# Two blocks of a network on one core: the feed-forward layer takes tokens before their norm, and three projections become split fp32r products

## The chip, the cores and the metric

The program runs on 1 core of a Trainium2 chip, as one launch. The metric is the device time in microseconds (us) of that core, as the median of several runs.

## The reference, cut to what matters

256 tokens of 1024 features go through two different blocks. The first block mixes tokens (a stick-breaking attention and a gated linear attention, called gla) and then has a convolutional feed-forward layer:

```
y = (jax.nn.sigmoid(gate_sb + b_gate[0]) * (o_sb @ w_branch_sb)
     + jax.nn.sigmoid(gate_gla + b_gate[1]) * (o_gla @ w_branch_gla))
h = h + y @ w_out                      # [256, 1024]
hn = rms_norm(h, norm_ffn_g)           # h * rsqrt(mean(h*h) + eps) * g, per token
u = hn @ w_ffn_in                      # [256, 2 * 2816]
a, g = jnp.split(u, 2, axis=-1)
a = causal_depthwise_conv(a, conv_w, conv_b)
h = h + (jax.nn.gelu(a) * g) @ w_ffn_out
```

The second block norms its input, projects it (`w_in_2`, a part of 416 columns called lat and a part of 512 columns called u), attends, and ends in a mixture of experts: 32 experts, the best 4 for each token, weights `w_gate_up_2` (8.4 MB an expert) and `w_down_2` (4.2 MB an expert), all in fp32.

## The kernel before, in words

Everything is written out by hand: each engine has its own program, and semaphores order them. `tensor_program` is TensorE's (PE), `vector_program` VectorE's (DVE), `scalar_program` ScalarE's (ACT), `gpsimd_program` GpSimd's (POOL), and `sync_program` issues the weight loads (SP). The weights of the first block and of the second block's projections come in pieces of 1 MB (128 x 2048 fp32) through a ring of 6 slots; a piece is loaded when the product that used the slot's last piece is done. Results are written to the 8 banks of PSUM in the order of the tables `RESULTS` and `RESULTS2`.

A *split product* replaces one fp32 product by three fp32r ones. ACT rounds the weights (`w_hi`, `ff_hi`), DVE or POOL subtracts to get what is left (`split_lo` into `ring_r`, `ffn_lo` into `ff_lo`), the same is done with the other operand, and PE adds hi*hi + hi*lo + lo*hi. Before the change the first 20 pieces (`SPLIT = 20`, the input projection) and the feed-forward layer are done so. The two branch projections (`branch(f, q)`, 8 column blocks `f` by 2 branches `q`, L1899) and the output projection (`project`, L1699) are plain fp32.

The stages around the change are, in time:

1. Branch projections from 152.8 us, gating into `y_T` on DVE (L1210 to L1213), output projection into banks `wo00` to `wo11`.
2. `h` gets the result (L1221), is transposed on PE (`turn_quarter`, banks `hT..`), drained with the gain (L1012). DVE and ACT form the mean of squares, POOL the reciprocal root. The factor of each token must be laid along the free dimension: DVE makes a diagonal (`h_diag`), PE multiplies it by ones (bank `rb1`), DVE multiplies `h_nT` by the bank (L1251), ACT rounds (`h_hi`, L809), DVE and POOL subtract (`h_lo`). `awake` issues 9 and then 6 matmuls that compute nothing, between these waits.
3. The feed-forward layer has 11 steps (`FF_STEPS`) of 256 columns. Step i needs `ffn_in("a", i)` and `ffn_in("g", i)` (48 matmuls of 256 columns each), then on ACT and DVE the chain pad, convolution (6 operations), gelu, product `ff_u`, `u_hi`, `u_lo`, and `ffn_out(i)` (24 matmuls of 512 columns into banks 0 to 3). PE's order in the loop is a(i+1), out(i), g(i+1).
4. After `ffn_out(10)` the four banks are added to `h`, transposed (`nT..`), and go through lat (2 x 8 matmuls of 416 columns) and u (32 of 256). The norm factor for u is broadcast through bank `rb` between lat and u. On ACT and DVE the lat values are scaled, their norms taken, and PE goes on with `qlT` when `lat_ready` says so.
5. Attention, router, and the experts. The first expert loads wait for results of the attention (L391: bank `pm1`).

Of the kernel before, what the change touches and what calls it, by code (L numbers as in the profile page):

```python
# [62 lines left out]
SPLIT = 20  # L63
# [159 lines left out]
def build(nc, w, out):  # L223
    with ExitStack() as ctx:
# [257 lines left out]
def gpsimd_program(g, pool):  # L482
# [146 lines left out]
def scalar_program(g, act):  # L629
# [31 lines left out]
    def w_hi(n):  # L661
# [126 lines left out]
    def ffn_step(i, q, turns, i0):  # L788
        pad(i, q)
        if i0 + 1 < FF_STEPS:  # L790
            ffn_hi("a", turns, i0 + 1)
        gelu(i, q)
        ffn_hi("o", turns, i0)
        if i0 + 1 < FF_STEPS:
            ffn_hi("g", turns, i0 + 1)
# [5 lines left out]
    act.wait_ge(s.y_ready, KT)  # L801
    ffn_hi("a", 0, 0)
    ffn_hi("g", 0, 0)
    square("ffn", *r1.drained("wo10"), scratch=t.ff_u[:].rearrange("p q k n -> p (q k n)"))
    act.preload_act_table(ACT.Gelu_apprx_tanh)
    for h in range(2):
        for b in range(NB):
            act.wait_ge(s.h_normed, 2 * h + b + 1)
            act.activation(h_part(t.h_hi, b, h), h_part(t.h_nT, b, h), ACT.Copy).then_inc(s.h_rounded, 1)  # L809
    act.wait_ge(s.ff_zero, 1)  # L810
# [149 lines left out]
def vector_program(g, dve):  # L960
# [228 lines left out]
    sb_out(1)  # L1189
    dve.wait_ge(*r1.drained("og1"))  # L1190
# [32 lines left out]
    def ffn_lo(kind, i, i0):  # L1223
# [3 lines left out]
        if i0 > 0:  # L1227
            dve.wait_ge(s.ff_a if kind == "a" else s.ff_o, i)
        dve.tensor_tensor(t.ff_lo[:, "ago".index(kind), :], t.ring[:, slot, :], t.ff_hi[:, slot, :].bitcast(F32),
                          ALU.subtract).then_inc(s.ff_lo_dve, 1)  # L1230

    add_mixed(0, 0)
    ffn_lo("a", 0, 0)
    add_mixed(0, 1)
    add_mixed(1, 0)
    for b in range(NB):
        turned("hT", t.h_nT, "norm_ffn", b, 0)
    add_mixed(1, 1)
# [1519 lines left out]
```

## Time and profile before

| | us |
|---|---|
| median of 3 runs | 1455.63 (1455.58 to 1460.12) |
| the profiled execution, its own time | 1460.94 |
| its span, first to last instruction | 1459.2 |
| PE busy in the span | 1386.4 |
| DVE, ACT, POOL busy | 676.2, 287.8, 518.4 |
| mean granted clock of TensorE | 0.989 of full |

The profile gives for the span busy time by engine, the chain of work that ended last, and groups of instructions; the trace below it gives each instruction. An fp32 matmul stands in PE's timeline as two records, an fp32r one as one. A start is in us from the first instruction of the span.

### The profile page before, as it was taken

What the parts mean: (1) busy time and instruction counts of PE and PEld (TensorE: products, weight loads), DVE (VectorE), ACT (ScalarE), POOL (GpSimd) and SP (SyncE); (2) the same over time, 40 slices, a digit from 0 to 9 for tenths busy, and PEclk for the clock granted to TensorE, in tenths of its full rate; (3) what the DMA queues carried; (4) which work ended last, traced back from release to release, by engine and by line L of the source; (5) the groups of instructions that cost most, each with busy time, mean ns of one, the idle gap of its engine ahead of it and who ended that gap; (6) DMA issues with size and microseconds to landing.
All of it is one profiled execution on the core that took longest, in us unless ns stands there. A gap on an engine that the chain in (4) does not pass through costs nothing.

```text
span 1459.2 us, 21155 instructions
## 1 busy us (share of the span) xinstructions
PE 1386.4 (95%) x7640; PEld 790.1 (54%) x7641; DVE 676.2 (46%) x1124; ACT 287.8 (20%) x445; POOL 518.4 (36%) x532
## 2 busy tenths in 40 slices
PE   8999999999989999999999999999998998999995
PEld 8899848999966753433433433433433333334332
DVE  7664436667646443433433433444434444333233
ACT  5644023444325300010100100000000000001001
POOL 3000012222233245565526556456654655200000
PEclk9999999999999999999999999999999999999998
DMA  9544254555545689999997999999999999999994
GB/s 312 174 145 134 98 173 145 177 196 174 187 147 198 259 346 390 429 429 426 429 428 309 430 427 428 427 429 428 428 427 428 429 426 429 427 429 428 428 427 199
DMA packets 77415, 480.76 MB, mean 329 GB/s; under 512 B 7019, under 2 KB 31272, under 8 KB 52808
## 3 DMA queue, kind: packets, MB, share of 16 engines
q1 hardware_dynamic: 74046, 477.45, 80.8%
q10 hardware_dynamic: 3338, 2.88, 0.7%
q8 instruction: 22, 0.36, 0.1%
q14 instruction: 9, 0.07, 0.0%
HBM read 479.26 MB, written 1.05 MB: 329 GB/s over the span
## 4 chain that ended last, share of the span: by engine, by line
PE 65%; DMA 30%; DVE 3%; issue 1%; ACT 1%; POOL 0%; SPq 0%; POOLq 0%; ACTq 0%; DVEq 0%
DMA ring_b<-in_w_down 22%; PE bank L2227 16%; PE bank L2303 12%; PE bank L1967 8%; PE bank L1749 6%; DMA ring<-in_w_gate_up 5%; PE bank L1979 4%; PE bank L1699 4%; PE bank L2209 2%; PE bank L1899 2%; DMA ring_b<-in_w_gate_up 2%; PE bank L1765 2%; PE bank L2262 1%; PE bank L1689 1%; PE bank L2051 1%
## 5 line engine op out<-in xcount | busy, mean ns | idle before, releaser
L619 POOL COPY ring<-stage 128x1024 f32<-128x1024 f32 x300 | 308.4, 1073 | 318.6 <-DMA stage<-in_w_gate_up 223.9
L2227 PE MATMUL bank<-ring,x_T 128*64 128x512 f32 x1584 | 356.0, 597 | 6.5 <-DMA ring<-in_w_gate_up 6.0
L2303 PE MATMUL bank<-ring_b,act_T 128*64 128x512 f32 x1056 | 244.3, 613 | 31.8 <-DMA ring_b<-in_w_down 31.3
L2227 PEld LDWEIGHTS bank<-ring,x_T 128*64 128x64 f32 x1584 | 112.6, 137 | 226.7 <-issue 210.9
L2303 PEld LDWEIGHTS bank<-ring_b,act_T 128*64 128x64 f32 x1056 | 77.9, 140 | 181.9 <-issue 154.1
L1569 DVE TENSOR_TENSOR h<-h,bank 128x512 f32<-128x512 f32 x128 | 82.3, 684 | 201.5 <-PE bank L2262 201.5
L1545 DVE SCALAR_TENSOR_TENSOR y_lo<-bank,slot_gate,y_hi 128x512 fp32r<-128x512 f32 x33 | 24.8, 751 | 226.3 <-ACT y_hi L900 226.3
L2227 PE MATMUL bank<-ring_b,x_T 128*64 128x512 f32 x528 | 120.6, 599 | 2.3 <-DMA ring_b<-in_w_gate_up 2.3
L914 ACT ACTIVATE sig<-bias_raw 128x512 f32<-128x512 f32 x33 | 20.8, 629 | 463.5 <-DVE bias_raw L1575 463.5
L619 POOL COPY ring_b<-stage_b 128x1024 f32<-128x1024 f32 x100 | 103.8, 1080 | 19.1 <-DMA stage_b<-in_w_gate_up 17.5
L544 POOL TENSOR_TENSOR ff_lo<-ring,ff_hi 128x2048 fp32r<-128x2048 f32 x11 | 51.0, 4640 | 157.8 <-PE bank L1967 111.1
L1967 PE MATMUL bank<-h_hi,ff_hi 128*128 128x256 f32 x352 | 99.9, 284 | 2.2 <-POOL h_lo L551 1.7
L1967 PE MATMUL bank<-h_lo,ff_hi 128*128 128x256 f32 x352 | 99.7, 283 | 0.0
L1967 PE MATMUL bank<-h_hi,ff_lo 128*128 128x256 f32 x352 | 99.7, 283 | 0.0
L900 ACT ACTIVATE y_hi<-bank,slot_gate 128x512 fp32r<-128x512 f32 x33 | 22.7, 687 | 274.5 <-PE bank L2303 274.5
L2227 PEld LDWEIGHTS bank<-ring_b,x_T 128*64 128x64 f32 x528 | 35.0, 136 | 71.3 <-issue 67.2
L624 POOL TENSOR_TENSOR bias_raw<-h,g_rows 128x1024 f32<-128x1024 f32 x1 | 2.4, 2361 | 193.2 <-DVEq L1637 193.2
L1967 PEld LDWEIGHTS bank<-h_hi,ff_hi 128*128 128x128 f32 x352 | 67.6, 192 | 3.1 <-issue 2.1
L786 ACT ACTIVATE ff_hi<-ring 128x2048 fp32r<-128x2048 f32 x33 | 61.8, 1903 | 34.4 <-DMA ring<-in_w_ffn_in 34.4
L2209 PE MATMUL bank<-picks,h_half 128*128 128x128 f32 x512 | 68.1, 287 | 0.0
L1967 PEld LDWEIGHTS bank<-h_lo,ff_hi 128*128 128x128 f32 x352 | 67.6, 192 | 0.4
L1967 PEld LDWEIGHTS bank<-h_hi,ff_lo 128*128 128x128 f32 x352 | 67.6, 192 | 0.0
(446 smaller groups left out, 1886.4 us busy)
## 6 DMA issues: line engine op xcount, KB each, us to landing
stage<-in_w_gate_up SPq DMA_DIRECT2D x75, 2048.0 KB, 24.6
ring_b<-in_w_down SPq DMA_DIRECT2D x64, 2048.0 KB, 23.3
stage_b<-in_w_gate_up SPq DMA_DIRECT2D x25, 2048.0 KB, 25.0
ring<-in_w_gate_up SPq DMA_DIRECT2D x21, 2048.0 KB, 25.0
ring<-in_w_in SPq DMA_DIRECT2D x22, 1024.0 KB, 5.1
ring<-in_w_ffn_in SPq DMA_DIRECT2D x22, 1024.0 KB, 5.1
ring_b<-in_w_gate_up SPq DMA_DIRECT2D x7, 2048.0 KB, 25.5
ring<-in_w_ffn_out SPq DMA_DIRECT2D x11, 1024.0 KB, 4.9
```

What stands on the lines that cost most here:

```text
L544: pool.tensor_tensor(t.ff_lo[:, 1, :], t.ring[:, slot, :], t.ff_hi[:, slot, :].bitcast(F32), ALU.subtract).then_inc(s.ff_lo_pool, 1)
L619: ins = pool.tensor_copy(pair_slot(g, pair)[:, cols], stage_place(g, pair)[:, cols])
L786: act.activation(t.ff_hi[:, n % RING, :], t.ring[:, n % RING, :], ACT.Copy).then_inc(s.ff_hi_done, 1)
L1569: dve.tensor_tensor(t.h[:, b, cols], t.h[:, b, cols], g.banks[2 + c][:], ALU.add).then_inc(s.added, 1)
L1699: ins = pe.matmul(bank[:, 0:n], src[:, k, b * P:(b + 1) * P], wk[:, c0:c0 + n], start=(k == 0), stop=(k == len(weights) - 1))
L1749: ins = pe.matmul(into[f // 2][:, (f % 2) * T:(f % 2 + 1) * T], wt[:, k, f * P:(f + 1) * P], xt[:, 4 * half + k, :], start=((half, part) = ...
L1765: ins = pe.matmul(into[b][:], xt[:, 4 * half + k, b * P:(b + 1) * P], wt[:, k, :], start=((half, part) == (0, 0) and k == 0), stop=((half, ...
L1967: ins = pe.matmul(bank[:, f * T:(f + 1) * T], wt[:, k, f * P:(f + 1) * P], ht[:, k, :], start=(k == 0 and part == 0), stop=(k == KT - 1 an ...
L1979: ins = pe.matmul(banks[2 * b + c][:], ut[:, q, k, b * P:(b + 1) * P], wt[:, k, 512 * c:512 * c + 512], start=False, stop=last, skip_group ...
L2209: ins = pe.matmul(banks[6][:, f * P:(f + 1) * P], t.h_half[:, b, k_rows], t.picks[:, b, :], start=(b == 0), stop=(b == 1))
L2227: ins = pe.matmul(banks[n][rows, :], t.x_T[:, c, :], job_slot(g, c)[:, c0:c0 + 512], start=False, stop=(c == GU - 1), skip_group_check=True)
L2303: ins = pe.matmul(banks[4][rows, :], t.act_T[:, k, SLOTS * (c // 2):SLOTS * (c // 2) + SLOTS], job_slot(g, GU + c)[:, c0:c0 + 512], start= ...
```

## The change: what it does

- **Split products for branches and output.** `SPLIT` becomes 28: pieces 20 to 27 are rounded on ACT (`w_hi`) and subtracted on DVE (`split_lo`). The activations are split as well: `o_hi`/`o_lo`, `gla_hi`/`gla_lo`, `y_hi_T`/`y_lo_T`, ACT rounding and DVE subtracting. PE does three fp32r products in place of each fp32 one. All first-branch blocks but two now come ahead of the transposes `ogt`.
- **Raw tokens.** `h_hi` and `h_lo` are made from `h_nT` without the token's norm factor. The factor is applied to a in the pad operation, which moves from ACT to DVE and multiplies by `h_scale` (a copy of bank `rb1`), and to g after `ffn_out`, when the rows are added to `h`. The diagonal product `rb1` moves in between the halves of the first `ffn_in` products. Both `awake` calls there go.
- **Loop order.** PE does a(i+1), g(i+1), out(i). DVE does `ffn_lo("a", i+1)` first in a step and `ffn_lo("o", i)` last.
- **End of the layer.** The last `ffn_out` is done bank by bank, with the first transposes between, lat starts before the last transpose, and bank `rb` comes between the halves of u.

```diff
-SPLIT = 20
+SPLIT = 28
...
+            act.wait_ge(s.w_split, n - HI + 1)
...
-    for n in range(4, 8):
-        gate(n)
+    gate(4)
+    gate(5)
+    w_hi(20)
+    o_high(0)
+    o_high(1)
+    w_hi(21)
+    gate(6)
+    gate(7)
+    w_hi(22)
     for b in range(NB):
         take(r1, f"og{b}", t.o_gla[:, b, :], r1.bank(f"og{b}")[:])
+    w_hi(23)
+    for n in range(2):
+        gla_high(n)
+    for f in range(3):
+        y_turned_high(f)
+    w_hi(24)
+    y_turned_high(3)
+    w_hi(25)
+    for f in range(4, KT):
+        y_turned_high(f)
+    w_hi(26)
+    w_hi(27)
...
     def ffn_step(i, q, turns, i0):
-        pad(i, q)
         if i0 + 1 < FF_STEPS:
             ffn_hi("a", turns, i0 + 1)
+            ffn_hi("g", turns, i0 + 1)
+        ffn_hi("o", turns, i0)
         gelu(i, q)
...
+        if f >= 1:
+            y_low(f - 1)
         dve.wait_ge(*r1.drained(f"y{f}"))
         dve.tensor_tensor(t.y_T[:, f, :], y_a, y_b, ALU.add).then_inc(s.y_ready, 1)
+    split_lo(24)
+    y_low(KT - 1)
+    split_lo(25)
...
+        if i0 + 1 < FF_STEPS:
+            ffn_lo("a", i + 1, i0 + 1)
+        dve.wait_ge(s.ff_a, i + 1)
+        dve.tensor_tensor(t.a_pad[:, q, :, 2:], g.banks[4 + q][:].rearrange("p (k n) -> p k n", k=2),
+                          t.h_scale[:].unsqueeze(1).to_broadcast([P, 2, T]), ALU.mult).then_inc(s.ff_pad, 1)
...
-        dve.tensor_tensor(t.h[:, b, cols], t.h[:, b, cols], g.banks[2 * b + n][:], ALU.add).then_inc(s.rows_added, 1)
+        dve.scalar_tensor_tensor(out=t.h[:, b, cols], in0=g.banks[2 * b + n][:], scalar=rstd("ffn", b),
+                                 in1=t.h[:, b, cols], op0=ALU.mult, op1=ALU.add).then_inc(s.rows_added, 1)
...
+        for part, (wt, xt) in enumerate(((w_hi, x_hi), (w_lo, x_hi), (w_hi, x_lo))):
+            if f == 0 and part != 1:
+                pe.wait_ge(s.o_rounded if part == 0 else s.o_split, 2 * q + 2)
+            if f % 4 == 0 and part < 2:
+                pe.wait_ge(s.w_rounded if part == 0 else s.w_split, n + 1)
...
+        into = [open_bank(r1, f"wo{col}{b}") for b in blocks]
+        for half, part in ((0, 0), (0, 1), (1, 0), (1, 1), (0, 2), (1, 2)):
+            w_hi, w_lo = split_parts(g, n + half)
+            wt, yt = ((w_hi, t.y_hi_T), (w_hi, t.y_lo_T), (w_lo, t.y_hi_T))[part]
+            if part == 0:
+                pe.wait_ge(s.w_rounded, n + half + 1)
+                pe.wait_ge(s.y_rounded, 4 * half + 4)
...
-            ffn_out(m * 2 + q, q, q)
             ffn_in("g", m * 2 + (q + 1), q + 1, banks[7 - q], s.ff_g)
-    ffn_out(FF_STEPS - 1, FF_STEPS - 1, 0, end=True)
+            pe.wait_ge(s.ff_u, m * 2 + (q + 1))
+            for b, c in QUARTERS:
+                ins = ffn_out(m * 2 + q, q, q, b, c)
+            ins.then_inc(s.ff_o, 1)
```

On PE, from the output projection to the first feed-forward matmuls, the program before reads as follows (`x_n` is the buffer of `y_T`; `ident` alone is an `awake` matmul):

```order
L1699 MATMUL bank<-ring,x_n 128x512 x24
L1677 MATMUL bank<-ident,h 128x128 x8
L1699 MATMUL bank<-ring,x_n 128x512 x8
L1708 MATMUL bank<-ident 128x128 x9
L1943 MATMUL bank<-h_diag,ones 128x128 x2
L1947 MATMUL bank<-zrow 128x512 x4
L1708 MATMUL bank<-ident 128x128 x6
L1967 MATMUL bank<-h_hi,ff_hi 128x256
```

The same place on PE in the changed program, from the second column half's first bank on:

```order
L1751 MATMUL bank<-ident,h 128x128 x8
L2018 MATMUL bank<-w_hi,y_hi_T 128x512 x4
L2018 MATMUL bank<-w_hi,y_lo_T 128x512 x4
L2018 MATMUL bank<-ring_r,y_hi_T 128x512 x8
L1751 MATMUL bank<-ident,h 128x128 x4
L2036 MATMUL bank<-zrow 128x512 x4
L2069 MATMUL bank<-h_hi,ff_hi 128x256 x8
L2069 MATMUL bank<-h_hi,ff_lo 128x256 x8
L2069 MATMUL bank<-h_lo,ff_hi 128x256 x8
L2095 MATMUL bank<-h_diag,ones 128x128 x2
```

The `h_diag` product stood between the output projection and the first feed-forward matmul; it now has three of the four half products (24 matmuls each) of step 0 ahead of it and one behind.

On DVE, where the gated `y` is made, one block `f` before:

```order
L1210 TENSOR_TENSOR gr_e<-bank,gates 128x256
L1211 TENSOR_TENSOR gr_e<-bank,gates 128x256
L1213 TENSOR_TENSOR x_n<-gr_e 128x256
L1214 MEMSET a_pad 128x516
L1215 MEMSET a_pad 128x516
```

and the last block with what follows it now (`y_lo_T` is the low part of the block before):

```order
L1268 TENSOR_TENSOR gr_e<-bank,gates 128x256
L1269 TENSOR_TENSOR gr_e<-bank,gates 128x256
L1260 TENSOR_TENSOR y_lo_T<-x_n,y_hi_T 128x256
L1273 TENSOR_TENSOR x_n<-gr_e 128x256
L1056 TENSOR_TENSOR ring_r<-ring,w_hi 128x2048
```

Each block has four operations in place of three, and weight subtractions stand behind the last.

On PE at the end of the feed-forward layer, before:

```order
L1979 MATMUL bank<-ff_hi,u_lo 128x512
L1677 MATMUL bank<-ident,h 128x128 x16
L1699 MATMUL bank<-ring,h_nT 128x416 x16
L2012 MATMUL bank<-diag,ones 128x128 x2
L1689 MATMUL bank<-h_nT,ring 128x256 x32
```

and now, behind the last quarter of `ffn_out`:

```order
L2081 MATMUL bank<-ff_hi,u_lo 128x512
L1751 MATMUL bank<-ident,h 128x128 x4
L2126 MATMUL bank<-ring,h_nT 128x416 x4
L1773 MATMUL bank<-ring,h_nT 128x416 x8
L2139 MATMUL bank<-h_nT,ring 128x256 x16
L2148 MATMUL bank<-diag,ones 128x128 x2
```

Two of the four transposes have moved ahead of the last quarter, one stands in the middle of the first lat product, and the `diag` product (bank `rb`) is half of u later.

## Rows read from the trace of the kernel before

**Rows 1.** The page: the chain that ended last by engine and line; bandwidth in 40 slices.

```profile
GB/s 312 174 145 134 98 173 145 177 196 174 187 147 198 259 346 390 429 429 426 429 428 309 430 427 428 427 429 428 428 427 428 429 426 429 427 429 428 428 427 199
...
PE 65%; DMA 30%; DVE 3%; issue 1%; ACT 1%; POOL 0%; SPq 0%; POOLq 0%; ACTq 0%; DVEq 0%
```

**Rows 2.** The chain in order of time: start, length, what (x: records).

```profile
36.42 11.09 PE bank L1765 x48
...
92.56 22.77 PE bank L1749 x192
...
160.84 20.72 PE bank L1899 x96
181.56 20.60 PE bank L1699 x48
...
255.79 5.47 PE bank L1979 x24
261.26 11.51 PE bank L1967 x96
...
405.17 7.35 PE bank L1979 x24
...
416.93 11.18 PE bank L1699 x32
428.55 13.81 PE bank L1689 x64
```

**Rows 3.** PE's timeline at the norm: start, busy, line, operation, idle ahead.

```profile
209.74 0.60 PE L1677 MATMUL bank<-ident,h 128*128 128x128 f32 x4
...
214.38 1.03 PE L1947 MATMUL bank<-zrow 1*128 1x512 bf16 x4
...
218.36 0.36 PE L1967 MATMUL bank<-h_hi,ff_hi 128*128 128x256 f32 x1 [1.41 <-POOL h_lo L551]
```

**Rows 4.** PE's timeline before the first and the last `ffn_out`.

```profile
238.59 0.47 PE L1979 MATMUL bank<-ff_hi,u_hi 128*128 128x512 f32 x1 [1.44 <-DVE u_lo L1282]
...
405.17 0.47 PE L1979 MATMUL bank<-ff_hi,u_hi 128*128 128x512 f32 x1 [2.31 <-DVE u_lo L1282]
```

**Rows 5.** Windows: length, busy of PE, PEld, DVE, ACT, POOL; clock, DMA.

```profile
236.00:239.00 3.00, 1.56 (x12) 1.34 (x11) 2.96 (x3) 1.81 (x2) 1.90 (x1) 1.00 0.19 32
...
407.00:410.00 3.00, 3.00 (x10) 2.40 (x9) 0.00 (x0) 0.00 (x0) 0.00 (x0) 0.64 0.00 0
```

**Rows 6.** DVE's timeline, the operations that the change repeats, adds or moves.

```profile
134.28 2.29 DVE L1019 TENSOR_TENSOR ring_r<-ring,w_hi 128x2048 fp32r<-128x2048 f32 x1 [1.63 <-ACT w_hi L667]
...
158.09 1.23 DVE L1199 TENSOR_TENSOR sb_s<-sb_s,rstd 128x1024 f32<-128x1024 f32 x1 [1.86 <-POOL rstd L503]
...
164.34 0.42 DVE L1210 TENSOR_TENSOR gr_e<-bank,gates 128x256 f32<-128x256 f32 x1 [2.60 <-PE bank L1899]
164.79 0.42 DVE L1211 TENSOR_TENSOR gr_e<-bank,gates 128x256 f32<-128x256 f32 x1
...
335.13 0.69 DVE L1279 TENSOR_TENSOR ff_u<-ff_ge,bank 128x512 f32<-128x512 f32 x1 [2.03 <-PE bank L1967]
336.52 3.74 DVE L1282 TENSOR_TENSOR u_lo<-ff_u,u_hi 128x512 fp32r<-128x512 f32 x1 [0.70 <-ACT u_hi L799]
```

**Rows 7.** POOL's timeline in the same loop step, and ACT's at 132 us.

```profile
335.09 4.62 POOL L544 TENSOR_TENSOR ff_lo<-ring,ff_hi 128x2048 fp32r<-128x2048 f32 x1 [12.36 <-PE bank L1967]
...
132.28 1.90 ACT L667 ACTIVATE w_hi<-ring 128x2048 fp32r<-128x2048 f32 x1
```

**Rows 8.** DVE's timeline after the last `ffn_out`.

```profile
412.54 1.88 DVE L1294 TENSOR_TENSOR h<-h,bank 128x512 f32<-128x512 f32 x3 [7.52 <-PE bank L1979]
...
425.93 0.48 DVE L1324 TENSOR_SCALAR diag<-ident,rstd 128x128 f32<-128x128 f32 x2 [2.77 <-POOL rstd L564]
...
437.73 0.35 DVE L1351 TENSOR_SCALAR lat_n<-lat,rstd 128x256 f32<-128x256 f32 x1 [4.30 <-POOL rstd L503]
```

**Rows 9.** SP's waits from 390 to 530 us: total, times, longest.

```profile
SPq L391 <- PE bank L2082: 10.2, 1, 10.2
```

More of the change, by code:

```diff
@@ L1934, in tensor_program @@
         turn_quarter(r1, "hT", t.h, b, 0)
-    project(r1, "wo11", 1, wo, t.y_T, 0, 512)
-    for b in range(NB):
-        pe.wait_ge(*r1.drained(f"wo1{b}"))
-        turn_quarter(r1, "hT", t.h, b, 1)
-    awake(9, 0)
+    mixed_out(1, (1,), 26)
+    pe.wait_ge(*r1.drained("wo10"))
+    turn_quarter(r1, "hT", t.h, 0, 1)
+    pe.wait_ge(*r1.drained("hT10"))
+    for n in range(4):
+        pe.matmul(banks[n][:], t.zrow[0:1, 0:P], t.zrow[0:1, P:], start=True, stop=False)
+    pe.wait_ge(*r1.drained("wo11"))
@@ new lines, in tensor_program, with ffn_parts, ffn_in @@
+    turn_quarter(r1, "hT", t.h, 1, 1)
+    def ffn_parts(kind, i, i0):
+        slot = ffn_chunk(g, kind, i0) % RING
+        pe.wait_ge(s.ff_lo_pool if kind == "g" else s.ff_lo_dve, ffn_made(kind, i)[1])
+        kt = 2 if kind == "o" else KT
+        return (t.ff_hi[:, slot, :].rearrange("p (k m) -> p k m", k=kt),
+                t.ff_lo[:, ffn_rest(kind, i0), :].rearrange("p (k m) -> p k m", k=kt))
+    def ffn_in(kind, i, i0, bank, done):
+        w_hi, w_lo = ffn_parts(kind, i, i0)
+        for f in range(2):
+            for k in range(KT):
+                for part, (wt, ht) in enumerate(((w_hi, t.h_hi), (w_hi, t.h_lo), (w_lo, t.h_hi))):
+                    ins = pe.matmul(bank[:, f * T:(f + 1) * T], wt[:, k, f * P:(f + 1) * P], ht[:, k, :],
+                                    start=(k == 0 and part == 0), stop=(k == KT - 1 and part == 2))
+        ins.then_inc(done, 1)
@@ new lines, in ffn_in_half @@
+    def ffn_in_half(kind, half, bank):
+        w_hi, w_lo = ffn_parts(kind, 0, 0)
+        for part, (wt, ht) in enumerate(((w_hi, t.h_hi), (w_lo, t.h_hi), (w_hi, t.h_lo))):
+            if kind == "a" and part == 0:
+                pe.wait_ge(s.h_rounded, 2 * half + 2)
+            if kind == "a" and part == 2:
+                pe.wait_ge(s.h_split, half + 1)
+                pe.wait_ge(s.h_split_pool, half + 1)
+            for f in range(2):
+                for k in range(4 * half, 4 * half + 4):
+                    ins = pe.matmul(bank[:, f * T:(f + 1) * T], wt[:, k, f * P:(f + 1) * P], ht[:, k, :],
+                                    start=(f == 0 and k == 0 and part == 0),
+                                    stop=(f == 1 and k == KT - 1 and part == 2), skip_group_check=True)
+        return ins
@@ new lines, in ffn_out @@
+    def ffn_out(i, i0, q, b, c):
+        w_hi, w_lo = ffn_parts("o", i, i0)
+        end = i0 == FF_STEPS - 1
+        for k in range(2):
+            for part, (ut, wt) in enumerate(((t.u_hi, w_hi), (t.u_hi, w_lo), (t.u_lo, w_hi))):
+                last = end and k == 1 and part == 2
+                ins = pe.matmul(banks[2 * b + c][:], ut[:, q, k, b * P:(b + 1) * P],
+                                wt[:, k, 512 * c:512 * c + 512], start=False, stop=last,
+                                skip_group_check=not last)
+        return ins
@@ L1940, in tensor_program @@
+    QUARTERS = [(b, c) for b in range(NB) for c in range(2)]
+    ffn_in_half("a", 0, banks[4])
+    pe.wait_ge(*r1.drained("hT11"))
+    ffn_in_half("g", 0, banks[6])
+    ffn_in_half("a", 1, banks[4]).then_inc(s.ff_a, 1)
     pe.wait_ge(s.h_diag_ready, NB)
@@ L1971, in ffn_out @@
-    def ffn_out(i, i0, q, end=False):
-        w_hi, w_lo = ffn_parts("o", i, i0)
-        pe.wait_ge(s.ff_u, i + 1)
-        for b in range(NB):
-            for c in range(2):
-                for k in range(2):
-                    for part, (ut, wt) in enumerate(((t.u_hi, w_hi), (t.u_hi, w_lo), (t.u_lo, w_hi))):
-                        last = end and k == 1 and part == 2
-                        ins = pe.matmul(banks[2 * b + c][:], ut[:, q, k, b * P:(b + 1) * P],
-                                        wt[:, k, 512 * c:512 * c + 512], start=False, stop=last,
-                                        skip_group_check=not last)
-        ins.then_inc(s.ff_o, 1)
```

253 lines of the change are left out of this document (151 added, 102 removed).

## The prediction

> **What bounds the kernel now.** I read the page first. The chain that ended last is 65% PE and 30% DMA [rows 1]. The bandwidth line shows where the two change places: up to the 12th of 40 slices (36.5 us each) the core draws 98 to 312 GB/s, from the 17th on it draws about 428 without a break, one slice excepted [rows 1]. So up to some 510 us the kernel is a chain of products, and behind that it is a stream of expert weights. The change lies wholly in the first part, from 152.8 to 442 us. Does a gain there reach the end? The first expert load waits for a bank of the attention (SP stood 10.2 us before it [rows 9]), so the start of the stream hangs on the front's chain. The stream then moves with it; I take 1 us at the end for 1 us at the front.
>
> Next I read the chain in order of time and PE's timeline beside it. Between 152.8 and 202 us PE is solid with fp32 products. Then come small waits at the norm, waits around the first `ffn_out`, a loop without idle time at 5.47 + 11.51 = 16.98 us a step [rows 2], a wait of 2.31 us before the last `ffn_out` [rows 4], and gaps around the transposes.
>
> **The cost of each product.** A branch matmul (fp32, 256 columns) takes 20.72 us for 96 records, which are 48 matmuls: 0.432 us. An output matmul (512 columns) takes 20.60/24 = 0.858. An fp32r matmul of 256 columns takes 22.77/192 = 0.119, one of 512 columns 11.09/48 = 0.231 [rows 2]. There are 64 branch matmuls and 32 output ones.
> Before: 64 x 0.432 + 32 x 0.858 = 55.1 us. After: 192 x 0.119 + 96 x 0.231 = 45.0. **Term 1: -10.1 us**, if the operands are there in time.
>
> **Are they?** Each of the eight added weight pieces costs ACT 1.90 [rows 7] and DVE 2.29 us [rows 6]. I walked through the changed programs with these durations. Pieces 20 to 22 fit into holes of ACT and DVE ahead of the gla norm, which starts when it did. It ends at 158.09 + 1.23 = 159.3 [rows 6]; PE now has six blocks (8.5 us) of the first branch ahead of the transposes and arrives at 161.3, so that wait stays covered. At the next two blocks PE waits some 0.6 us for banks that the transposes used.
> Then the gating. DVE starts two operations 0.45 us apart [rows 6]. A block had three, 1.37 us, and has four, 1.83. PE fills a bank every 12 x 0.119 = 1.42 us. Before, PE was slower than DVE (1.73 a block); now DVE is slower. It starts block 0 at 167.0 (after subtracting piece 23) and ends block 7 at 181.8; ACT rounds it until 182.4. PE has its branches done at 176.9, does the two parts of the output product that need only the first half of y (3.7 us, to 180.6) and waits until 182.4. **Term 2: +1.9 us for this wait and +0.6 for the banks.** The low part of block 7 comes behind a weight subtraction (184.5), just where PE wants it. Pieces 26 and 27 are subtracted by 192.6, PE wants the latter at 194.8: covered, by 2 us. If it weren't, `add_mixed` on DVE would be late next, and with it the transposes.
>
> **The norm.** Before, the output products end at 209.74, where the transposes of `h` begin, and the first feed-forward matmul is at 218.36 [rows 3]: 8.6 us, in which lie the mean, POOL's root, `rb1`, the scaling, the rounding and the subtraction. After, PE ends the output products at 202.3 by the sum so far. Behind them stand four transposes (0.43), four `zrow` matmuls (about 0.9, their row's 1.03 less the overlap [rows 3]) and four transposes: the first feed-forward half product starts at 204.1, 1.8 us later. Its first three parts need the tokens' first half, whose low part POOL has at about 203.5. **Term 3: -6.8 us.** The norm's own chain (mean, root, diagonal) ends near 210 on DVE, and PE asks for it at 212.6, behind three half products of 2.85 us: covered by 2.6 us. If that cover were gone, each us late would count, since the loop's pad needs it.
>
> **The loop.** A step keeps its 120 matmuls, so 16.98 us while PE bounds it. What must not happen is that DVE needs more. Its step is now: `ffn_lo("a")` 2.29 (the size of a weight piece), pad 0.7 (a 512-element row that reads a bank), convolution 3.1 (six of 256), wait for gelu 0.7, product 0.7, wait for `u_hi` 0.7, `u_lo` 0.7, `ffn_lo("o")` 2.29: 11.2 us [rows 6]. To that comes a wait for POOL. The row of `u_lo` shows it: 3.74 us for 512 elements, started at 336.52 while POOL's subtraction ran from 335.09 to 339.71; the product ahead of it, which reads a bank, took 0.69 beside the same POOL operation [rows 6, 7]. So a DVE operation that reads two buffers of SBUF ends only behind POOL's. That can add at most 4.6: 15.8 of 16.98. The loop stays PE's. The Trainium skill (GPSIMD Engine Reference, section 1, Specifications) says that POOL shares its SBUF interfaces with VectorE, and that they contend when the DVE instruction has two SBUF inputs; the trace agrees. By the rule alone, without the row's length, a convolution and two weight subtractions in a step are exposed beside `u_lo`, and the loop could be slowed; by the row they have 1.2 us of room.
>
> Ideal is 11 x 16.98 = 186.8 us from the first feed-forward matmul to the end of the last `ffn_out`. Before it took 412.54 - 218.36 = 194.2, that is 7.4 more: waits before `ffn_out(0)` (1.44) and `ffn_out(10)` (2.31) [rows 4], the latter's 24 matmuls at 7.35 in place of 5.47 [rows 2] because the granted clock was 0.64 at 407 us [rows 5] (between the two levels of 1.2 and 2.4 GHz, after that pause), and smaller ones. After: `rb1` 0.5; two transposes inside the last `ffn_out` 0.9; and at the start a stall. DVE gets to `ffn_lo("a", 1)` only behind the copy of `rb1`, so the first step's convolution runs into POOL's subtraction and the first `ffn_out` waits. I get 1.2 us, and between 0 and 1.3 more at the next a: take 1.5, bounds 0 and 3. Then `ffn_out(10)` has 5.47 us of `ffn_out(9)` ahead, against a chain of 4.7. So 2.9 more than ideal. **Term 4: -4.5 us.**
>
> **The end of the layer.** From the end of `ffn_out(10)` (412.54) to the end of u (428.55 + 13.81) were 29.8 us [rows 2, 8]. After the last quarter PE now has: transpose 0.43, lat 11.2, transpose 0.43, u 13.8, `rb` 0.45 = 26.3 [rows 2]. The mean for the second norm needs all rows added; it is at 425.93 - 412.54 = 13.4 us before and about 12.7 after, and `rb` stands at 19.4: fine. But the broadcast `rb` is also what DVE waits for ahead of the lat norms, since its copy comes first in its order: 19.5 in place of 16. The lat values were scaled by four operations from 437.73 on [rows 8], ready at about 438.7, 26.2 us after the layer's end, set by constants that POOL makes ahead of its root. I get 25.5 now, 0.8 before PE asks. **Term 5: -3.5 us**; if DVE's lat chain is slower by more than 0.8, the excess comes off.
>
> **Sum.** -10.1 + 2.5 - 6.8 - 4.5 - 3.5 = -22.4. The profiled execution took 1460.94 us, so its like would be 1438.5; it lies 5.3 above the median of 1455.63, so I put the median at **1433.5 us**.
>
> **The rivals.**
> *Less is kept (0.28).* PE pauses and its clock falls. The `awake` matmuls are gone; a pause of 2.31 us was followed by clock 0.64, one of 1.44 us was not [rows 4, 5]. My waits of 1.9 us at the y stage lie between. A drop costs what the last `ffn_out` shows, 7.35 - 5.47 = 1.9 us. With two drops, 1.5 us more at the start of the loop and 2 us more in DVE's gating (each block 1.83 plus a quarter for semaphores) 22.4 shrinks to 15: 1441. The Trainium skill (TensorE: Matmul & The Clock Gate, Part 1) has the clock fall after the engine idled and advises against gaps; by it removing the filler is a risk only where waits stay, which here is the one place. The sum by it is 1.9 less.
> *More is kept (0.04).* No stall in the loop, no wait at y because DVE's operations close up: 26 to 28 us, 1428.
> *The stream doesn't follow (0.04).* If the weights' stream and not the front sets the end, some or all is lost: 1450 to 1456. Against it: SP's wait for the attention's bank [rows 9], and 259 to 390 GB/s in slices 14 to 16, which is not the stream's full rate [rows 1].
> *Slower (0.04).* The loop becomes DVE's. If POOL held up DVE twice in a step (convolution and `ffn_lo`), the step would be 11.2 + 2 x 4.6 = 20.4 us, 3.4 above PE's; over 10 steps 34 us, less the 22.4: +12, 1468. It decides from 2.2 us a step on. Against it: POOL has one subtraction a step, so it can hold DVE once.
> *The forecast itself* (17 to 26 us kept): 0.60.
>
> **How the numbers follow.** About 0.3% (4.4 us) is what a measurement tells from no change. Faster by more than that: 0.60 + 0.28 + 0.04 and half of the stream's case, 0.94. Slower: 0.04; the same: 0.02. The range reaches from "more is kept" to the lesser gain, 1428 to 1441, which leaves out about 0.15 (the outer ends of these two, the stream and the slower case) and takes in the bounds of the stall (0 to 3) and of the y wait (0 to 4).
>
> **What would show it.** In the profile of the changed kernel: fp32r rows of 0.119 and 0.231 us at the branches and the output; a pause of about 2 us on PE near 181 with y's rounding as releaser; the first feed-forward matmul near 204; a step of 16.98 us; the last `ffn_out` straight behind the one before; end of u near 420. It is wrong if the step is longer than 17 us, if the clock is below 1.00 between 180 and 220 us, if PE waits for `lat_ready`, or if the first expert load isn't 22 us earlier.

## The result, and the profile after

| | before | after |
|---|---|---|
| median of 4 runs, us | 1457.2 (1455.58 to 1460.12) | 1438.93 (1436.48 to 1441.42) |
| profiled execution, us | 1460.94 | 1438.70 |
| its span, us | 1459.2 | 1437.0 |
| mean granted clock | 0.989 | 0.987 |

The ratio is 0.9859, with a 95% interval from 0.9838 to 0.9879: 18 to 24 us less. Forecast were 1433.5 us, a range of 1428 to 1441, and 22.4 us less. The median lies in the range. The medians themselves differ by 18.3 us (a quotient of 0.9875, inside the interval); below, the effect by the ratio is 20.5 us and by the two spans 22.2. A second series of five runs of the same kernel (`e1_again`, below) gave 1434.76 (1432.71 to 1437.86), against 1459.68 for the kernel before in the same session. The two series' intervals overlap by little; the mean clock of the runs was 0.986 to 0.990 in the first and 0.989 to 0.994 in the second.

The page of the changed kernel, the lines that answer to [rows 1]:

```profile
GB/s 316 172 148 121 133 191 149 197 196 188 183 186 253 274 355 402 427 428 428 429 368 365 429 428 427 429 427 428 428 427 429 428 426 428 429 427 429 429 428 198
...
PE 65%; DMA 30%; DVE 2%; ACT 1%; issue 1%; POOL 0%; SPq 0%; POOLq 0%; DVEq 0%; ACTq 0%
```

The picture is the old one: a chain of products and then a stream of some 428 GB/s. So I read where the chain stands. Its pieces in order of time (start, length, what), as in [rows 2]:

```profile
152.42 8.65 PE bank L1980 x72
161.07 0.45 PE bank L1995 x4
...
162.29 14.35 PE bank L1980 x120
176.64 17.05 PE bank L2018 x72
193.69 0.87 PE bank L1751 x8
194.56 5.60 PE bank L2018 x24
...
202.15 8.64 PE bank L2069 x72
...
379.77 9.55 PE bank L2081 x42
389.32 0.87 PE bank L1751 x8
390.19 1.40 PE bank L2081 x6
...
403.64 6.91 PE bank L2139 x32
410.55 0.44 PE bank L2148 x4
410.99 6.91 PE bank L2139 x32
417.90 0.44 PE bank L2156 x4
```

Branch products (L1980) and output products (L2018) stand one behind the other without a hole but one of 0.35 us at 162. The last two `ffn_out` have become one piece from 379.77. The end of u is at 417.90; before, it was at 428.55 + 13.81 = 442.36 [rows 2]. That is 24.5 us earlier, and the span is only 22.2 shorter. (0.4 of the 24.5 was there before the changed part began: the branch products start at 152.79 us before and at 152.35 after.) PE's timeline behind that point, before the change, then after it, and in the second profile of the same changed kernel:

```profile
484.15 5.57 PE L2124 MATMUL bank<-v_tok,prob_T 128*128 128x64 f32 x48 [0.97 <-ACT prob_T L656]
...
518.05 5.35 PE L2227 MATMUL bank<-ring,x_T 128*64 128x512 f32 x16 [0.41 <-DVE x_T L1520]
```

```profile
459.68 8.50 PE L2259 MATMUL bank<-v_tok,prob_T 128*128 128x64 f32 x48 [0.97 <-ACT prob_T L662]
...
497.80 3.65 PE L2362 MATMUL bank<-ring,x_T 128*64 128x512 f32 x16 [0.41 <-DVE x_T L1594]
```

```profile
459.68 5.57 PE L2259 MATMUL bank<-v_tok,prob_T 128*128 128x64 f32 x48 [0.97 <-ACT prob_T L662]
...
493.59 3.65 PE L2362 MATMUL bank<-ring,x_T 128*64 128x512 f32 x16 [0.41 <-DVE x_T L1594]
```

The same 48 matmuls behind the same pause of 0.97 us take 5.57 us or 8.50. The windows from 462 us on say why; the number before the DMA share is the granted clock. First the changed kernel, then its second profile:

```profile
462.00:464.00 2.00, 2.00 (x12) 2.00 (x11) 0.48 (x1) 0.00 (x0) 0.00 (x0) 0.50 0.40 164
```

```profile
462.00:464.00 2.00, 2.00 (x21) 2.00 (x19) 0.47 (x1) 0.00 (x0) 0.00 (x0) 1.00 0.38 156
```

Clock 0.50 is the lower of the two levels (1.2 GHz). It lasted from 462 to 472 us and cost 497.80 - 493.59 = 4.2 us. In the profile before, the clock fell later instead: the first expert product took 5.35 us in place of 3.65. So of the 24.5 us 4.2 were lost here and 1.7 won back by that accident: 22.0 at the expert stage, and 22.2 at the end. The fall at the av products is not the change's doing: the second profile of the same kernel has the same pause and no fall. The fall in the profile before lies behind the changed part, and one profile of that kernel is all there is.

The last sign that the prediction named is the first expert load. The loads that SP issued for the experts, before and after:

```profile
412.92 0.43 SPq L394 DMA_DIRECT2D stage_b<-in_w_gate_up  x1
...
459.83 0.34 SPq L391 DMA_DIRECT2D ring<-in_w_gate_up  x1
```

```profile
392.01 0.44 SPq L399 DMA_DIRECT2D stage_b<-in_w_gate_up  x1
...
435.36 0.34 SPq L396 DMA_DIRECT2D ring<-in_w_gate_up  x1
```

The load that waits for the attention's bank came 24.5 us earlier. It is the second expert load and not the first, as I had written: the first goes out when the last `ffn_out` is done, 20.9 us earlier than before.

### The profile page after: what moved, and what is told of

It is laid out like the page before. It is cut to its first block, busy times and chain, and to the rows that moved or that the text cites. A ratio compares the mean times of both kernels' runs of the same rounds, so it can differ in the third digit from the quotient of the medians.

```text
span 1437.0 us, 21298 instructions
## 1 busy us (share of the span) xinstructions
PE 1371.5 (95%) x7706; PEld 791.9 (55%) x7707; DVE 719.9 (50%) x1152; ACT 302.0 (21%) x454; POOL 523.5 (36%) x532
## 4 chain that ended last, share of the span: by engine, by line
PE 65%; DMA 30%; DVE 2%; ACT 1%; issue 1%; POOL 0%; SPq 0%; POOLq 0%; DVEq 0%; ACTq 0%
DMA ring_b<-in_w_down 23%; PE bank L2362 16%; PE bank L2438 12%; PE bank L2053 7%; PE bank L1823 6%; DMA ring<-in_w_gate_up 5%; PE bank L2081 4%; PE bank L2344 2%; DMA ring_b<-in_w_gate_up 2%; PE bank L1773 2%; PE bank L1980 2%; PE bank L2018 2%; PE bank L1839 2%; PE bank L2397 1%; PE bank L2139 1%; PE bank L2186 1%
## 5 line engine op out<-in xcount | busy, mean ns | idle before, releaser
L2053 PE MATMUL bank<-h_hi,ff_hi 128*128 128x256 f32 x320 | 90.6, 283 | 0.0
L2053 PE MATMUL bank<-h_lo,ff_hi 128*128 128x256 f32 x320 | 90.5, 283 | 0.0
L2053 PE MATMUL bank<-h_hi,ff_lo 128*128 128x256 f32 x320 | 90.5, 283 | 0.0
L1056 DVE TENSOR_TENSOR ring_r<-ring,w_hi 128x2048 fp32r<-128x2048 f32 x28 | 64.2, 2301 | 27.1 <-ACT w_hi L674 27.0
L2344 PEld LDWEIGHTS bank<-picks,h_half 128*128 128x128 f32 x512 | 62.8, 196 | 0.8 <-issue 0.8
L2053 PEld LDWEIGHTS bank<-h_hi,ff_hi 128*128 128x128 f32 x320 | 61.4, 192 | 0.5 <-DVE ff_lo L1292 0.2
```

The source lines that it names most:

```text
L1056: dve.tensor_tensor(t.ring_r[:, n % RING, :], t.ring[:, n % RING, :], t.w_hi[:, n % HI, :].bitcast(F32), ALU.subtract).then_inc(s.w_split, 1)
L2053: ins = pe.matmul(bank[:, f * T:(f + 1) * T], wt[:, k, f * P:(f + 1) * P], ht[:, k, :], start=(k == 0 and part == 0), stop=(k == KT - 1 an ...
L2344: ins = pe.matmul(banks[6][:, f * P:(f + 1) * P], t.h_half[:, b, k_rows], t.picks[:, b, :], start=(b == 0), stop=(b == 1))
```

## The experiments

All are edits of the changed kernel. "e1" is its second profile; starts are compared with those of e1 after the start of the branch products (152.39 us in e1) is made equal. A ratio is to the kernel before, with runs of the same session. "Clock falls" means that the granted clock went from 1.00 to 0.50.

**The unedited kernel again (e1_again).** No edit.

> The changed kernel, unedited, for a second profile and a closer ratio. Theory A (the drop of the granted clock to 0.50 between 462 and 472 us is an accident of one execution, since the program before has the same pause of 0.97 us there at clock 1.00): the drop may be absent, the av products then take 5.6 and not 8.5 us, and the end of the front is 24.5 us earlier than before and not 21.9. Theory B (it comes with this program's times): it is there again, L2259 takes 8.5 us. Ratio to the kernel before 0.984 to 0.988 in both.

Measured: 1434.76 us, ratio 0.9832 [0.9817, 0.9846]; in the profile no window of 4 us up to 600 us has a granted clock below 1.00. Theory A holds: the fall comes in some executions and not in others. Against the profile before, each piece from the end of u to the start of the first expert product is 24.5 us earlier, the expert stages are 26.1 earlier (the 1.7 us above), and the spans differ by 1459.2 - 1433.0 = 26.2: what the front gains, the end gains, 1 us for 1 us. The five runs range over 5 us, and the fastest two have the highest mean clock (0.994; the slowest 0.989).

**A filled pause (e2_fill_av).**

```diff
+    bank = open_bank(r2, "av0")
+    for _ in range(6):
+        pe.matmul(bank[:, 0:P], t.ident[:], t.ident[:], start=True, stop=True)
     pe.wait_ge(*r2.drained("pt7"))
```

> Six matmuls that compute nothing (128x128, about 0.15 us each) stand where PE waits 0.97 us for prob_T ahead of the av products. Theory A (the clock falls because of this pause): clock 1.00 from 455 to 480, av products 5.6 us in place of 8.5, and the first expert product 4.2 us earlier than in the profile of the changed kernel; the time falls by 2.5 to 4.2 us against it. Rival B (the pause is too short to matter, the fall has another cause): the fall is still there, time unchanged. Rival C (the experts' stream decides): front earlier, end unchanged.

Measured: 1434.94 us, ratio 0.983 [0.9817, 0.9842]: no gain over e1. The six matmuls took 1.34 us together, 0.22 each and not 0.15, so they fill the pause and hold PE 0.2 us longer. The clock stayed at 1.00 at the av products and fell later. Windows of this kernel:

```profile
462.00:464.00 2.00, 2.00 (x21) 2.00 (x19) 0.69 (x1) 0.00 (x0) 0.00 (x0) 1.00 0.55 221
...
486.00:488.00 2.00, 2.00 (x6) 1.64 (x5) 0.82 (x2) 1.23 (x1) 0.00 (x0) 0.50 1.04 438
...
496.00:498.00 2.00, 2.00 (x8) 0.89 (x6) 0.01 (x1) 0.00 (x0) 0.00 (x0) 0.50 0.96 410
```

At 486 us PE was busy through the window, behind router products of 32 columns and transposes; the last pause ahead of it, at 482 us, was 0.25 us. Twelve profiles of the changed kernel and its variants were taken. The fall at the av products, behind the pause of 0.97 us, came in five of ten without the filler and in neither of the two with it (e2 and e10), but both of these fell at about 484 and 494 us instead. Theory A's price (2.5 to 4.2 us less) is refuted. Whether the pause brings the fall is not shown: at five in ten, two profiles without a fall there come by chance one time in four. The Trainium skill (TensorE: Matmul & The Clock Gate, Part 1) has the clock fall after idle time; here a fall came behind 0.97 us of it in some executions and not in others, and at 484 us with hardly any.

**g's subtraction from POOL to DVE (e3_dve_g, e9_dve_g2).** In e3 it stands behind `u_lo`, in e9 ahead of the product `ff_u` (shown):

```diff
-    with pool.Fori(0, (FF_STEPS - 1) // 2) as m:
-        ffn_lo(m * 2 + 1, 1)
-        ffn_lo(m * 2 + 2, 2)
...
         dve.sem_inc(s.ff_conv, 1)
+        if i0 + 1 < FF_STEPS:
+            slot = ffn_chunk(g, "g", i0 + 1) % RING
+            dve.wait_ge(s.ff_hi_done, ffn_made("g", i + 1)[0])
+            dve.wait_ge(s.ff_g, i + 1)
+            dve.tensor_tensor(t.ff_lo[:, 1, :], t.ring[:, slot, :], t.ff_hi[:, slot, :].bitcast(F32),
+                              ALU.subtract).then_inc(s.ff_lo_pool, 1)
```

> From step 1 of the loop on, the subtraction for g stands on DVE (behind u_lo) and not on POOL. Theory (the loop is PE's; POOL holds a DVE operation up by about 4 us once in a step, which DVE's spare time takes up): no DVE operation of the convolution is longer than 0.5 us, the step stays 16.98 us, only the 0.8 us before the first ffn_out goes; 0 to 1 us less in all. Rival (DVE is the bound of the step): with 2.29 us more of its own work and no hold-up the step changes, to less than 16.9 if POOL's hold-up set it, or to more than 17.1 if DVE's own work does.

> As e3_dve_g, but DVE's subtraction for g stands between the convolution and the product, so that the first step's g doesn't wait for u_lo. Theory (in e3 only the first step lost time: PE asked for g's low part 2.7 us before it was there; afterwards the loop is PE's): it is there at about 220.3 us, when a(1) ends, the first ffn_out starts without idle time, 0.5 us earlier than in the changed kernel, and the step stays 16.98. So the first expert product comes 0.5 us earlier at clock 1.00, and the time is that of the unedited kernel within 1 us, as far as clock falls let one see it. Rival (DVE's place in the step matters for the loop as well): steps over 17.0 us.

Measured: e3 1441.53 us, ratio 0.9872 [0.9857, 0.9886]; e9 1434.37, ratio 0.982 [0.9807, 0.9834]. The step is 16.98 us in both: the loop is PE's, with the hold-ups and without. My "0 to 1 us less" for e3 was wrong: g's low part for step 1 now came behind `u_lo`, and PE waited 2.60 us for it; the first `ffn_out` is 2.0 us later. The rest of what e3's median has over e1's goes with the clock (0.987, a fall at the av products in its profile). In e9 that wait is gone, and so are the 0.80 us before the first `ffn_out`: the front is 0.7 us shorter than in e1, which the medians can't tell apart. DVE's timeline, the changed kernel's first, third and fourth step and its wait in a later one, then e9's first:

```profile
213.93 0.69 DVE L1332 TENSOR_TENSOR a_pad<-bank,h_scale 128x512 f32<-128x512 f32 x1
214.66 4.37 DVE L1339 TENSOR_SCALAR ff_c<-a_pad,vec_T 128x256 f32<-128x256 f32 x1
...
244.10 4.75 DVE L1339 TENSOR_SCALAR ff_c<-a_pad,vec_T 128x256 f32<-128x256 f32 x1 [0.30 <-DVE a_pad L1332]
...
261.52 4.61 DVE L1341 SCALAR_TENSOR_TENSOR ff_c<-a_pad,vec_T,ff_c 128x256 f32<-128x256 f32 x1 [0.15 <-DVE ff_c L1341]
...
306.20 2.29 DVE L1292 TENSOR_TENSOR ff_lo<-ring,ff_hi 128x2048 fp32r<-128x2048 f32 x1 [1.02 <-PE bank L2053]
```

```profile
214.08 0.68 DVE L1329 TENSOR_TENSOR a_pad<-bank,h_scale 128x512 f32<-128x512 f32 x1
214.80 0.41 DVE L1336 TENSOR_SCALAR ff_c<-a_pad,vec_T 128x256 f32<-128x256 f32 x1
```

With POOL at rest the `TENSOR_SCALAR` takes 0.41 us, beside POOL's subtraction (214.25 to 218.87) it ends only behind it. From the fourth step on it is mostly a `SCALAR_TENSOR_TENSOR` that meets POOL's subtraction (4.61 us in place of 0.48). At 306.20 DVE waits 1.02 us for PE, and in the steps behind it again 0.9 to 1.0: that is the room that the loop has. Between 254.95 and 302.89, where DVE never waits for PE, its steps are 15.9, 16.2 and 15.9 us.

**POOL's work twice (e11_pool_twice).** Behind its subtraction POOL subtracts in a buffer of its own, in steps 1 to 8; nobody reads it. (Its loop is cut short by one round, and the last two subtractions stand behind it.)

```diff
+        if i0 in (1, 2):
+            pool.wait_ge(s.spare_done, i)
+            pool.tensor_tensor(t.spare[:], t.spare[:], t.spare[:], ALU.subtract).then_inc(s.spare_done, 1)
```

> POOL has a second subtraction of the same size (on a buffer that nobody reads) behind its own in steps 1 to 8 of the loop. Theory (a DVE operation that reads SBUF waits for the end of a POOL operation that is under way, so two in a row hold DVE up twice): DVE's step is 11.2 plus twice some 4.2, 19.6 us, above PE's 16.98; eight steps are 19 to 20.5 us long and the layer ends 17 to 28 us later. Rival (the second finds DVE waiting for PE or ACT anyway, or on operations that read banks): step 16.98, no loss.

Measured: 1449.11 us of 2 runs, ratio 0.9917 [0.9896, 0.9938]; the layer ends 11.9 us later. The steady step is 18.2 us; PE waits for DVE in it, and DVE never for PE. DVE's, POOL's and PE's timelines in one such step:

```profile
269.41 3.74 DVE L1346 TENSOR_SCALAR ff_c<-a_pad,vec_T 128x256 f32<-128x256 f32 x1 [0.28 <-DVE a_pad L1339]
273.30 3.59 DVE L1348 SCALAR_TENSOR_TENSOR ff_c<-a_pad,vec_T,ff_c 128x256 f32<-128x256 f32 x1
...
267.09 5.91 POOL L549 TENSOR_TENSOR ff_lo<-ring,ff_hi 128x2048 fp32r<-128x2048 f32 x1 [8.79 <-ACT ff_hi L830]
272.96 3.65 POOL L553 TENSOR_TENSOR spare<-spare 128x2048 f32<-128x2048 f32 x1
...
302.82 0.49 PE L2088 MATMUL bank<-ff_hi,u_hi 128*128 128x512 f32 x1 [0.98 <-DVE ff_lo L1299]
```

The mechanism of the "slower" rival is shown: two POOL operations, two DVE operations held up (3.74 and 3.59 us), and DVE bounds the step. The size was less than I expected (19.6) for two reasons in the rows: POOL's added operation takes 3.65 us, not 4.6, and its first had run for 2.3 us when DVE's convolution came. So this kernel doesn't give the room in the unedited loop; the changed kernel's own rows do: a DVE step of 15.9 to 16.2 us, against the 15.8 that I forecast, and 0.8 to 1.1 us of room.

**The loop's old order (e4_order).**

```diff
             ffn_in("a", m * 2 + (q + 1), q + 1, banks[5 - q], s.ff_a)
-            ffn_in("g", m * 2 + (q + 1), q + 1, banks[7 - q], s.ff_g)
             pe.wait_ge(s.ff_u, m * 2 + (q + 1))
             for b, c in QUARTERS:
                 ins = ffn_out(m * 2 + q, q, q, b, c)
             ins.then_inc(s.ff_o, 1)
+            ffn_in("g", m * 2 + (q + 1), q + 1, banks[7 - q], s.ff_g)
```

DVE's `ffn_lo("o", i)` also moves back, ahead of the wait for gelu.

> The loop's old order on PE, a(i+1), out(i), g(i+1), with DVE's subtraction for o ahead of gelu; all else stays. Theory (term 4: the new order gives the chain behind g the products of a and g as cover): steps stay 16.98 us, but the first ffn_out waits some 5 us in place of 0.8, and the last some 2.3 us in place of 0, with up to 2 us of low clock behind either: +7 to +11 us. Rival (the order is worth nothing, the saving in term 4 came from the earlier conv): within 2 us.

Measured: 1451.98 us, ratio 0.9936 [0.9921, 0.9952]; the layer ends 11.5 us later, and the first expert product is 16.9 later, since the clock falls at the av products too. PE's timeline before the first and the last `ffn_out`, and then two windows behind them (clock: the third number from the end):

```profile
226.27 0.79 PE L2081 MATMUL bank<-ff_hi,u_hi 128*128 128x512 f32 x1 [6.02 <-DVE u_lo L1352]
...
395.01 0.80 PE L2081 MATMUL bank<-ff_hi,u_hi 128*128 128x512 f32 x1 [2.22 <-DVE u_lo L1352]
```

```profile
226.00:229.00 3.00, 2.73 (x7) 2.18 (x8) 1.89 (x2) 3.00 (x3) 0.00 (x0) 0.50 0.00 0
...
395.00:398.00 3.00, 2.99 (x7) 2.41 (x8) 0.00 (x0) 0.54 (x1) 0.00 (x0) 0.50 0.51 201
```

The waits are 6.02 and 2.22 us in place of 0.80 and 0, 7.4 more, and the remaining 4 are the two stretches at half clock. The theory holds, at the upper end and half a us above. The edit undoes both orders at once: `u_lo` of the first step is 1.6 us later than in e1 because DVE's `ffn_lo` now stands ahead of it, so some 4.4 of the 6.02 are PE's order by itself (an estimate; no run parts them).

**The norm's product first (e5_norm_first).** The block of `rb1` (wait for `h_diag_ready`, two matmuls) moves ahead of `ffn_in_half("a", 0, ...)`.

> The product h_diag (bank rb1) stands ahead of the first half product of the feed-forward layer, as before the change; the tokens stay raw. Theory (term 3: what is saved is that PE doesn't wait for the norm's chain): PE waits from 201.9 to 207.1 us, 5.2 us; 0.8 of it comes back at the first ffn_out, whose chain starts earlier; if the clock falls behind the pause, up to 1.9 more. +4.4 to +6.3 us at the end. Rival (the saving is in the removed fillers and the broadcast multiply, not in the wait): +1 us or less.

Measured: 1442.18 us, ratio 0.9888 [0.9861, 0.9915]; the first expert product is 7.0 us later. PE's timeline:

```profile
206.97 1.22 PE L2091 MATMUL bank<-h_diag,ones 128*128 128x128 f32 x4 [4.96 <-DVE h_diag L1318]
207.84 2.06 PE L2069 MATMUL bank<-h_hi,ff_hi 128*128 128x256 f32 x8
```

Eight matmuls take 2.06 us in place of 1.20: the granted clock is 0.52 at 204 to 206 us and 0.50 from 206 to 210, in and behind the pause of 4.96 us. The wait and the fall are what the cover saves. The 0.8 us did not come back: DVE's first operation of the step, `ffn_lo("a", 1)`, waited at 218.20 for the end of a(0), whose low part lies in the same buffer, and no longer for `rb1`.

**The end of the layer as before (e6_tail_old).** All quarters, four transposes, lat, `rb`, u.

> The end of the layer in the old order: all four quarters of the last ffn_out, then four transposes, lat, bank rb, u. Theory (term 5, -3.5, less the 0.9 us that two transposes inside the last ffn_out cost in term 4): +2.6 us. Rival (rb's place is what counts, since DVE waits for it ahead of the lat norms): PE waits for lat_ready or diag_ready between lat and qlT, and the chain from the layer's end to the end of u stays at 26.3.

Measured: 1437.75 us, ratio 0.9854 [0.9833, 0.9874]; the first expert product is 1.3 us later, not 2.6. Its chain in order of time:

```profile
380.08 10.91 PE bank L2081 x48
390.99 0.45 PE bank L1751 x4
...
393.47 0.66 PE bank L1751 x4
394.12 5.59 PE bank L2122 x16
```

From the layer's end to the first lat product it takes 3.1 us; before the change it took 4.4 (412.54 to 416.93 [rows 2]). What is left of the change there is that the banks are still added to `h` one by one, each behind its own quarter, an edit that I hadn't undone and hadn't priced apart. So of term 5 and the 0.9 us in term 4 (2.6 together), 1.3 is the moved transposes and `rb`, as this run shows; that the other 1.3 is the adding by quarters is read from the two chains, and no run undoes it.

**A fifth operation in each gating block (e7_spare_op).**

```diff
+        dve.tensor_tensor(t.spare[:, f % 2, :], t.gates[:, f, :], t.gates[:, KT + f, :], ALU.mult)
         if f >= 1:
             y_low(f - 1)
```

> DVE has one more 128x256 operation in each of the eight gating blocks; it writes to a buffer that nobody reads. Theory (the wait of 1.9 us forecast at y was absent only because DVE's four operations take 1.46 us a block, starting 0.33 us apart, and not the 1.83 that I assumed): a block takes about 1.8 us, DVE is the bound of this stage, y's rounding ends near 182 and PE waits 1.3 to 2.1 us for it; +1.3 to +2.1 us, plus up to 1.9 if the clock falls behind it. Rival (the stage has slack elsewhere): no wait, time unchanged.

Measured: 1438.93 us, ratio 0.9857 [0.9836, 0.9878]; the first feed-forward product is 1.4 us later. A block is now 170.07 to 171.87 = 1.80 us, almost the 1.83 that I had forecast for four operations. (The median is 4.2 us above e1's; in the profile the clock falls at the av products.) PE's timeline of this kernel:

```profile
181.61 2.10 PE L2019 MATMUL bank<-w_hi,y_hi_T 128*128 128x512 f32 x8 [1.24 <-ACT y_hi_T L785]
```

Here is the wait that the prediction had placed at 180.6, with the releaser that it named.

**Plain fp32 at branches and output (e8_fp32).** `SPLIT = 20`, fp32 products in `branch` and `project`, and none of the roundings and subtractions that they no longer need.

> Branch and output projections as plain fp32 products again, with their weight and activation splits gone from ACT and DVE; all else stays. Theory (term 1: fp32 is 0.432 and 0.858 us a matmul, three fp32r ones 0.357 and 0.693): +10.1 us less 0.35 for a wait at the transposes that goes: +9.7, and the end of the kernel moves by the same. Rival (the splits on DVE and ACT eat a part): +5 to +8. Rival (the stream doesn't follow the front): the end of u is 9.7 later, the end of the kernel less.

Measured: 1446.92 us, ratio 0.9913 [0.9894, 0.9931]; the first feed-forward product is 10.0 us later and the end of u as well. The theory holds. The first expert product is 15.5 us later in its profile (clock falls at 472, 500 and 510 us), so the median tells less here than the timeline.

**e9 and the filler together (e10_best).**

> e9 and the six filler matmuls of e2 together. Theory: front 0.5 us shorter and no fall of the clock at the av products (which five of nine profiles with that pause show, 4.2 us each): 1433 to 1435 us, ratio 0.981 to 0.983. Rival (falls come later instead, as in e2 at 484 and 494 us): no better than the unedited kernel.

Measured: 1435.72 us (1431.97 to 1438.99), ratio 0.9821 [0.98, 0.9841]: no better than e1 or e9. The rival holds: the falls came at 484 and 494 us, as in e2. By its front e9 is the best of all kernels run, by 0.7 us that only the trace shows.

## Why the prediction came out as it did

The effect was 22.2 us by the profiles, 20.5 by the ratio and 18.3 by the medians, forecast 22.4; with the clock's accidents taken out, up to the end of u, it is 24.5, of which 0.4 lies ahead of the changed part. So the terms together came to 24.1 where the forecast has 22.4, and that the two spans differ by 22.2 is luck: the wait of 1.9 us that never came nearly cancels with the 2.5 us of clock (4.2 lost, 1.7 won back). Point by point:

- **Term 1, -10.1.** Right. 72 branch matmuls in 8.65 us are 0.120 each, 24 output matmuls in 5.60 are 0.233, and e8 shows the whole at 10.0. The stage from the first branch product to the end of the output products took 200.00 - 152.35 = 47.65 us, before 209.74 - 152.79 = 56.95: 9.3 less, which is 10.1 - 0.8 (term 2).
- **Term 2, +2.5.** The 0.6 for the transposes' banks was right: from 161.52 to 162.29 the chain runs over DVE, 0.8 us. The 1.9 for y was wrong: there was no wait. The step that failed reads "DVE starts two operations 0.45 us apart. A block had three, 1.37 us, and has four, 1.83". DVE's timeline of the changed kernel:

```profile
169.69 0.42 DVE L1268 TENSOR_TENSOR gr_e<-bank,gates 128x256 f32<-128x256 f32 x1
170.15 0.42 DVE L1269 TENSOR_TENSOR gr_e<-bank,gates 128x256 f32<-128x256 f32 x1
170.49 0.42 DVE L1260 TENSOR_TENSOR y_lo_T<-x_n,y_hi_T 128x256 fp32r<-128x256 f32 x1
170.82 0.42 DVE L1273 TENSOR_TENSOR x_n<-gr_e 128x256 f32<-128x256 f32 x1
171.15 0.42 DVE L1268 TENSOR_TENSOR gr_e<-bank,gates 128x256 f32<-128x256 f32 x1
```

  From block to block it is 1.46 us: 0.46, and then 0.34, 0.33 and 0.33. Before, the sum of two products waited for the second of them and started 0.46 us behind it; `y_lo_T`, which needs neither, stands in that gap now. The fourth operation cost 0.09 us, not 0.46. PE fills a bank in 1.42 us, so DVE fell behind by little and PE went from L1980 to L2018 without a wait. It was close: ACT ends the last rounding of y (`y_hi_T`, from 179.66 us on) at 180.08, and PE takes it at 180.22. e7 shows that the rest of the step (the wait, its place, its releaser) was right once a block takes 1.80 us.
- **Term 3, -6.8.** Right: 200.00 to 201.90 is 1.9 us in place of 8.6, so -6.7. The norm's chain ended at 207.1, PE asked at 210.6: 3.5 us of cover. e5 shows what it is worth, 7.0 us with the clock.
- **The loop.** Right: 16.98 us a step, PE's. A DVE step is 15.9 to 16.2 us, forecast 15.8. But my rule for POOL, "a DVE operation that reads two buffers of SBUF", was too narrow. In the first steps the operation held up is a `tensor_scalar` with one tensor, 0.41 us by itself and 4.37 beside POOL; in the later ones it is a `scalar_tensor_tensor` with two. The Trainium skill (SBUF — State Buffer, section "Who interferes with whom") says that `tensor_scalar` and `copy` can take the shared pair (the SBUF ports that VectorE and GpSimd share) as well, and that whoever comes first keeps it for the whole instruction; the trace agrees, in the other direction too (POOL's operation took 5.91 us in place of 4.62 in e11, where it started during one of DVE's own subtractions).
- **Term 4, -4.5.** Right: 201.90 to 391.59 is 189.7 us in place of 194.2. The stall before the first `ffn_out` was 0.80, forecast 1.2, and there was no second; I had taken 1.5 for both, and smaller gaps that I had put at nothing made up the 0.7, so that the sum hits to 0.1 is luck in part. The prediction names the copy of `rb1` and POOL's hold-up of the convolution as the stall's reason. It is the hold-up: with the copy 10 us ahead of DVE's `ffn_lo` (e5, 208.23 and 218.20) the stall stays, without the hold-up (e9) it is gone.
- **Term 5, -3.5.** Right: 391.59 to 417.90 is 26.3. `lat_n` was ready at 417.0, 0.9 us before PE asked. Which edit brings what I had not said; e6 does, for half of it.
- **The stream follows 1:1.** Right: 26.2 at the end for 26.1 at the first expert stages (e1). Backwards, too: e6's front is 1.7 us later than e1's and its span 1.1 longer; e8's 15.2 and 17.0, e4's 17.0 and 18.6, both with a first expert product of 5.35 us in place of 3.65. Only e5 looks like an exception, 6.8 and 4.5 (all these without the correction of the start); its last expert product took 7.11 us and e1's 8.76, which is 1.7 of the 2.3.
- **Less is kept, by the clock.** The place was wrong, the kind right. Neither profile of the changed kernel has a fall between 180 and 420 us. One came behind the pause of 0.97 us at the av products, which the change doesn't touch.

The absolute number missed for another reason. I took 5.3 us off because one profiled run of before lay above the median of three. In the later sessions that kernel's medians were 1459.68, 1459.01 and 1460.75: the profiled 1460.94 was the better base, and 1438.5, which the prediction gave for "its like", is 0.4 us from the median measured first (and 3.7 from e1's).

## What to carry to other kernels

Price an added operation by where it stands between two that depend on each other: in the gap of a wait for a result it is nearly free. Before a product is taken off the chain, look which of its operands is ready last; here three half products cover the 5 us that PE would wait for the norm's chain, and moving one block back ahead of them costs 7 us. And where single executions differ by 5 us with the clock, judge an edit of 1 us by the starts in the trace, stage by stage, and not by medians.

## What the hardware showed that I had not expected

- A DVE operation waits out a POOL subtraction even if it reads one tensor: a `tensor_scalar` on SBUF of 256 fp32 elements took 4.37 us beside a POOL subtraction and 0.41 without it. One with a PSUM bank as the other input is not held up (`ff_u`, 0.69 us beside POOL in the kernel before and 0.69 alone in the changed one).
- A DVE operation of 0.42 us starts 0.33 us behind one that it doesn't depend on, and 0.46 us behind one whose result it needs.
- The granted clock fell behind a pause of 0.97 us in five of the ten profiles of the changed kernel and its variants that have it, and not in the profile before; in e2 it fell at 484 us, where the 18 us ahead have pauses of 0.34 and 0.25 us, and in e11 at 454 us, 10 us behind one of 0.62. What decides between falling and not stays open.
